# Slot two's weights behind the first gathers, and a new order around the first two expert slots

## The reference

```python
gl = (x @ p['w_rg']).astype(jnp.float32) + p['b_rg'].astype(jnp.float32)
gp_sel, gsel = lax.top_k(jax.nn.softmax(gl, axis=-1), 1)
el = (x @ p['w_re']).astype(jnp.float32) + p['b_re'].astype(jnp.float32)
...
topv, topi = lax.top_k(ep, TOP_K_IN_GROUP)
...
g = jnp.einsum('nd,edf->nef', x, p['w_e_gate'])
u = jnp.einsum('nd,edf->nef', x, p['w_e_up'])
act = jax.nn.silu(g) * u * combine[:, :, None]
out = jnp.einsum('nef,efd->nd', act, p['w_e_down'])
```

## Time and profile before

| | us |
|---|---|
| median of 3 runs | 731.97 (730.36 to 732.15) |
| the profiled execution, whole | 733.88 |
| its span in the trace | 732.0 |
| TensorE busy in it | 696.0 (95%) |
| VectorE, ScalarE, GpSimd busy | 540.6, 346.7, 211.5 |

### The profile page before, as it was taken

The page is one execution under the profiler, slowest core; times in us unless marked ns, Lnnn a source line. Parts: engine busy times, 40 slices in busy tenths (PEclk is TensorE's granted clock), DMA queues, the critical chain, the costliest instruction groups (busy, mean ns, idle before and its releaser), DMA issues.

```text
span 732.0 us, 11123 instructions
## 1 busy us (share of the span) xinstructions
PE 696.0 (95%) x4409; PEld 606.8 (83%) x4409; DVE 540.6 (74%) x782; ACT 346.7 (47%) x455; POOL 211.5 (29%) x89
## 2 busy tenths in 40 slices
PE   5899999999999999999999999999879999999985
PEld 2489989999898898999999999887358888887762
DVE  3546999999858865865465564556789999878887
ACT  4542232432333443555276031125468888777644
POOL 3004323222200000000000000000129999889486
PEclk9899999999999999999999999999799999999998
DMA  9944244555615357441133434375948999989865
GB/s 321 377 149 145 83 173 173 173 174 186 233 57 91 49 124 127 34 144 58 60 120 96 143 115 138 121 259 203 420 166 332 397 404 409 419 325 383 322 240 205
DMA packets 75607, 149.10 MB, mean 204 GB/s; under 512 B 11302, under 2 KB 54626, under 8 KB 68836
## 3 DMA queue, kind: packets, MB, share of 16 engines
q1 hardware_dynamic: 61572, 125.28, 50.1%
q10 hardware_dynamic: 10096, 12.63, 4.8%
q0 software_dynamic: 3888, 10.49, 4.1%
HBM read 138.29 MB, written 20.05 MB: 216 GB/s over the span
## 4 chain that ended last, share of the span: by engine, by line
PE 57%; DVE 22%; DMA 8%; issue 5%; POOL 4%; ACT 2%; SPq 2%; POOLq 0%; DVEq 0%; ACTq 0%
PE psum L1015 19%; DVE psum L2095 14%; PE psum L1291 8%; PE psum L1333 7%; DMA down_raw<-in_w_e_down 4%; PE psum L514 3%; PE psum L515 3%; PE psum L520 3%; PE psum L950 3%; DMA w_more<-in_w_ada 2%; DMA xg<-h_d,slot_b 2%; PE psum L1034 1%; PE psum L1167 1%; SPq L813 1%; POOL down_l L732 1%
## 5 line engine op out<-in xcount | busy, mean ns | idle before, releaser
L1015 PE MATMUL psum<-hh,w_h 128*128 128x320 f32 x608 | 145.1, 320 | 0.2 <-issue 0.2
L1015 PE MATMUL psum<-hl,w_h 128*128 128x320 f32 x608 | 138.9, 310 | 0.0
L1015 PE MATMUL psum<-hh,w_l 128*128 128x320 f32 x608 | 138.8, 310 | 0.0
L1015 PEld LDWEIGHTS psum<-hh,w_h 128*128 128x128 f32 x608 | 100.1, 189 | 6.1 <-issue 3.6
L2095 DVE SCALAR_TENSOR_TENSOR psum<-conv,taps,psum 128x760 f32<-128x760 f32 x100 | 101.5, 1015 | 3.4
L1015 PEld LDWEIGHTS psum<-hl,w_h 128*128 128x128 f32 x608 | 102.0, 188 | 0.0
L1015 PEld LDWEIGHTS psum<-hh,w_l 128*128 128x128 f32 x608 | 102.0, 189 | 0.0
L698 POOL TENSOR_TENSOR ob<-obh,toff 128x260 bf16<-128x260 f32 x1 | 2.0, 1994 | 331.8 <-DVE obh L606 331.8
L732 POOL TENSOR_TENSOR down_l<-down_raw,down_h 128x2048 fp32r<-128x2048 f32 x16 | 87.1, 5444 | 21.7 <-ACT down_h L1851 21.4
L2386 DVE TENSOR_TENSOR w_l<-w_raw,w_h 128x2048 fp32r<-128x2048 f32 x26 | 76.0, 2927 | 12.4 <-ACT w_h L1857 12.4
L942 POOL TENSOR_TENSOR w_l<-w_raw,w_h 128x2048 fp32r<-128x2048 f32 x9 | 42.1, 4680 | 142.3 <-ACT w_h L1532 142.3
(11 more groups left out here) (384 smaller groups left out, 1397.8 us busy)
## 6 DMA issues: line engine op xcount, KB each, us to landing
w_raw<-in_w_in SPq DMA_DIRECT2D x20, 1024.0 KB, 6.3
down_raw<-in_w_e_down SPq DMA_DIRECT2D x17, 1024.0 KB, 16.5
w_raw<-in_w_ada SPq DMA_DIRECT2D x16, 1024.0 KB, 9.7
w_raw<-in_w_e_gate SPq DMA_DIRECT2D x13, 1024.0 KB, 9.0
w_raw<-in_w_e_up SPq DMA_DIRECT2D x13, 1024.0 KB, 11.7
w_more<-in_w_ada SPq DMA_DIRECT2D x8, 1024.0 KB, 10.0
y_d<-yy ACTq DMA_DIRECT2D x15, 512.0 KB, 8.1
y_d<-in_x_sample SPq DMA_DIRECT2D x12, 512.0 KB, 8.8
```

The costliest lines, as they stand in the source:

```text
L1015: mm = pe.matmul(psum[:, p + q, 0:HALF], w, r[:, k, q * HALF:(q + 1) * HALF], start=(k == 0 and x == 0), stop=(k == KT - 1 and x == 2))
```

## The change

Six edits, all around the first slots:

1. SyncE: slot 2's gate and up weights are asked for after the `h2` stores and after both first gathers have landed, where they were asked for ahead of the down weights of slots 1 and 0. Slot 2's down weights follow them, so they now wait for the gathers too.
2. TensorE, slot 0: the rows of slot 1 are turned after slot 0's sixteen high products, where they were turned before them.
3. ScalarE: one Silu on a constant right after the router's two exponentials, and slot 1's two high weights ahead of the copies of `bg2`, where they were made inside slot 0.
4. VectorE: slot 0's second low weight after the two `x_low`, and slot 1's first low weight ahead of slot 1's `x_low`.
5. VectorE: the reduction to `wslot` stays ahead of slot 0 (`late_weights`); the thirteen other instructions of `late_tables` run after slot 0.
6. The count of slots is announced by the second step of semaphore `tables`.

```diff
+    def late_weights(dve):
+        dve.wait_ge(rt_pe, 3)
+        dve.tensor_reduce(wslot[:, :], psum[:, 6, 4 * NS:7 * NS].rearrange("p (k n) -> p n k", k=3), AX, ADD).then_inc(tables, 1)
+        dve.wait_ge(tables, 1)
+
     def late_tables(dve, then):
...
-        dve.wait_ge(rt_pe, 3)
-        then(dve.tensor_reduce(wslot[:, :], psum[:, 6, 4 * NS:7 * NS].rearrange("p (k n) -> p n k", k=3), AX, ADD))
         then(dve.scalar_tensor_tensor(out=pair_of(6), in0=pair_of(2), scalar=float(CAP), in1=places, op0=MUL, op1=ADD))
...
# SyncE
-        gate_up(2, 0, own(2))
         sp.wait_ge(x2_done, NT)
         down_weights(1, 1, own(1))
         sp.wait_ge(lg_done, 1)
         down_weights(0, 0, own(0))
         sp.wait_ge(h2_st, 16 * (NT + 1))
+        for s in range(2):
+            sp.wait_ge(xg_in[s], 16)
+        gate_up(2, 0, own(2))
         down_weights(2, 0, own(2))
...
# TensorE, slot
-            if not last:
+            if not first and not last:
                 turn_x(1 - s, u + s, b + 1)
...
             with_high(pe, psum[:, s, :], [(xh[:, s, k, :], xl[:, s, k, :], both(wh, k)) for k in range(KT)])
+            if first:
+                turn_x(1, 0, 1)
             pe.wait_ge(e_lo, 2 * b + 2)
...
# ScalarE
+        act.activation(rms[:, 31:32], ones[:, 0:1], ACT.Silu)
         gate2_rows(1)
+        for c in range(2):
+            w_hi(1, 1, 0, c)
...
-            if not last:
+            if early > 0 and not last:
                 for c in range(2):
                     w_hi(1 - s, b + 1, u + s, c)
...
# VectorE
-        for c in range(2):
-            w_lo(0, 0, c)
+        w_lo(0, 0, 0)
         x_low(0, 0, 0)
         x_low(0, 0, 1)
-        late_tables(dve, then)
+        w_lo(0, 0, 1)
+        late_weights(dve)
...
+            if early == 0:
+                w_lo(1, 1, 0)
             if not last:
                 for q in range(2):
                     x_low(1 - s, b + 1, q)
+            if early > 0 and not last:
                 w_lo(1 - s, b + 1, 0)
...
-        for b in range(LOOP_AT):
+        slot(0, 0, 0)
+        late_tables(dve, then)
+        for b in range(1, LOOP_AT):
             slot(b, b % 2, b // 2)
```

More of the change, by code:

```diff
@@ L668, in pair_count @@
     def pair_count(eng):
-        eng.wait_ge(tables, 1)
+        eng.wait_ge(tables, 2)
         return eng.value_load(pairs_i[0:1, 0:1], min_val=0, max_val=(OVER - 1) // 2) + NE // 2
```

## The result

The changed kernel takes 735.27 us (median of 5 runs, 734.44 to 740.83) where the kernel before takes 730.70 (5 runs, 730.26 to 732.15): a ratio of 1.0087, 95% interval 1.0064 to 1.0109, slower by 4.6 us. 737.5 had been forecast, slower with 0.76.

A forecast was written before the change was run, and what follows sets the result against it. TensorE, busy 95%, was taken as the bound, with VectorE and GpSimd excluding each other in slots 1 and 2. 7.0 - 2.95 + 1.5 = 5.55 us slower gave 739.4 profiled, 737.5 on the 731.97 median; range 731.0 to 740.3.

The forecast's parts named there:

- The hold: Behind slot 0, GpSimd's down-weight subtraction goes first and holds the first of VectorE's thirteen table instructions until S + 7.61.
- S: Start of slot 0's Silu on ScalarE: 545.54 us before, predicted 2.95 us earlier, at 542.6.
- two operands in SBUF: Reason given for the hold: tiny VectorE instructions reading two SBUF operands wait for GpSimd's subtraction, as at 694.45 (3.42 us).
- GpSimd's second subtraction: For slot 1, ready at S + 10.2, goes ahead of VectorE's first low weight of slot 2, until S + 14.8.
- 7.0: Loss in us at slot 1's activation turns on TensorE, against S: S + 17.4 instead of S + 10.41.
- No further loss from slot 3 on: Sign that the prediction is right: the slots from 3 on lose nothing more.
- The gather's 2.5 us: First gather lands at 533.2 instead of rows reaching TensorE at 535.75: gain 2.5 us, bounds nothing to 2.86.
- The turns behind the products: Slot 0 on TensorE: 1.1 us saved by turning slot 1's rows later, 0.9 coming back between high and low products.
- The clock's 1.5 us: TensorE's clock falls to 0.50 somewhere between 553 and 565 us, costing 1.5 us.
- two waits that were predicted: TensorE idle about 2.8 us ahead of slot 0's down products and about 4 us ahead of slot 1's activation turns.
- the rival without a hold: Tiny instructions aren't held behind slot 0, TensorE bounds, full 2.95 us gained: 729.0 us; chance 0.14.
- 4.05 + 1.5: Whole predicted loss, 5.55 us: 7.0 lost against S less its 2.95 gain, plus 1.5 for the clock.

The follow-up runs named there:

- GpSimd after the tables: Changed kernel, with GpSimd's first subtraction for the down weights made to wait until the thirteen table instructions are done: 734.81 us, ratio 1.0078.
- only the tables moved: Kernel before, with only the thirteen table instructions moved behind slot 0 (and edit 6, which goes with it): 737.27 us, ratio 1.0110.
- only weights moved: Kernel before, with only slot 2's three weights asked for behind the first gathers: 730.26 us, ratio 1.0015.
- six tables late: Changed kernel, with seven table instructions ahead of slot 0's first turns and six (a reduction, a minimum, four casts) behind slot 0: 731.77 us, ratio 1.0033.
- down weight late: Kernel of tables in the wait, with slot 2's gate and up weights asked for at their old place again: 730.55 us, ratio 0.9997.
- seven products: Kernel of tables in the wait, plus seven products of constants on TensorE ahead of slot 0's first product: 732.64 us, ratio 1.0033.
- tables in the wait: Changed kernel, with the thirteen table instructions back ahead of slot 0's products, between its first low weight and low tokens: 730.72 us, ratio 1.0017.
- clock at the products: Kernel of down weight late, plus five products of constants while TensorE waits for the rounded rows ahead of slot 0's first product: 730.64 us, ratio 1.0002.
- four casts late: Changed kernel, with nine table instructions ahead of slot 0's first turns and only the four casts behind slot 0: 733.22 us, ratio 1.0034.

## Why the prediction was right, and where it was not

1. **The hold, the step on which the sign rested: right.** The first of the thirteen lasted 4.56 us instead of 0.17 and ended with GpSimd, the tables were done at S + 10.03 (S + 10.15 predicted). The two runs that put only these instructions in the one place or the other move the time by 4.5 us (changed kernel) and 6.9 us (kernel before). Freeing these instructions of the hold is not enough, though: in the run with GpSimd after the tables they weren't held, two low weights were, and the loss stayed. The reason given, two operands in SBUF, was too narrow: a minimum with a constant and a cast were held as well, a reduction was not. The Trainium skill ("SBUF — State Buffer", section "SBUF: two separate sides") names VectorE instructions in a two-port mode beside those with two SBUF inputs, and I had used only the second. That the minimum and the cast were held (4.28 and 4.61 us) fits the first, but no row here shows in which mode they ran.

2. **GpSimd's second subtraction: the right collision at the wrong instruction.** Predicted ahead of slot 2's first low weight, slot 1's turns then at S + 17.4. In the run with only the tables moved it is so (S + 17.30). In the changed kernel slot 1's products began later, behind the third gather, and at a clock of 0.58 (see 5.); slot 1's Silu came at S + 10.24 instead of S + 7.9, and VectorE had begun the first low weight when GpSimd was ready. Slot 1's turns came at S + 14.21; the second low weight was held instead (6.30 us), and slot 2's turns came at S + 26.14, 6.40 us later than before against S (566.64 - 540.50, and 565.28 - 545.54 before; the row of 565.28 is):

```profile
565.28 0.39 PE L950 MATMUL psum<-ident,act 128*128 128x128 f32 x2
```

7.0 had been predicted, for slot 1's turns, which were only 3.80 late. "No further loss from slot 3 on" holds, but slot 2 itself had its share.

3. **The gather's 2.5 us: mis-sized.** The first turns came 1.02 us earlier against G (5.63 after it, 6.65 before). The gather was no longer the last to come: TensorE's own eight products of the scale rows took 6.33 us at the clock of 0.50, and the turns waited 0.47 us for what ScalarE makes of them. Before, the clock rose at 530 us, in the midst of these products, and they took 4.96; after, the low stretch was longer, 13.7 us instead of 10.2 (515.3 to 529.0, and 519.6 to 529.9), for a reason that no run shows. In other kernels of this set these products took 4.92 to 5.50 us, and the first turns came 4.56 to 4.84 us after G (only weights moved, six tables late, down weight late, seven products): 1.8 to 2.1 of the 2.5 us were there to be had. I had taken the landing of the gather for the wait's end, and not asked what else would be late by then.

4. **The turns behind the products: right.** From the first turns to S it is 9.79 us before and 9.41 after; 0.45 less was predicted with the clock. With 3., S gains 1.40 us instead of 2.95.

5. **The clock's 1.5 us: at the wrong place.** No low stretch came between 553 and 565 us; TensorE's waits from 550 to 567 us were 0.22, 0.76, 1.14 and 0.87 us. (Of the two waits that were predicted, 2.8 and 4.2 us, the first wasn't longer than both of those seen before, as the text has it: one of them is 2.86.) It came at 542 to 546 us, behind the wait for slot 0's activation and a third gather 0.52 us late. That gather was issued at 533.01, among slot 2's 3 MB (issued from 532.67 to 533.94), and took 9.4 us to land; the prediction had the lateness of the weights in view, at no cost, and not that of the gather beside them. The low clock's cost lay largely beside the hold: TensorE waited 0.22 us for `al` where 2.8 was predicted.

The sum at slot 2 is 6.40 - 1.40 = 5.00 us, 4.05 + 1.5 = 5.55 in the prediction; at slot 12 4.29 is left, at the end 4.44. That the two sums lie so close is luck in part: the clock's 1.5 us, which didn't come where they were placed, stand in the sum for the 1.55 us of S's gain that stayed out. The forecast of 737.5 came from 731.97 for the kernel before; on the 730.70 of the longer comparison the same sum gives 736.25, 1 us above what was measured. That the rival without a hold was given 729.0 (the full gain of S kept) was wrong too: the run with the tables in the wait is the nearest to that case, and kept nothing of it that can be measured.

What stays open: what takes, between slot 9 and the end, the lead of 1.5 to 2.3 us that three of the kernels with unheld tables have at slot 2 (tables in the wait, only weights moved, clock at the products). The waits speak for transfers taking part up to slot 12; behind slot 16 something else takes the lead, and what that is isn't shown.

## What to carry to other kernels

Here small bookkeeping instructions on VectorE cost only their own length where GpSimd wasn't at a long subtraction from SBUF, and the rest of that subtraction where it was. Put them into a wait of VectorE, and look at which instruction of GpSimd becomes ready just before the place. When a transfer is moved to make another arrive earlier, find the second-latest thing that the waiting instruction needs, since the gain ends there. And a lead at the start of a pipeline need not reach its end: read the waits of the later slots, and of what follows them, before adding it to the sum.

## What the runs showed of the hardware that was not expected

- One-operand VectorE instructions of 128x10 and 128x16 elements, a minimum with a constant and a cast to int32, are held by GpSimd's subtraction for 4.28 and 4.61 us; a reduction from SBUF beside the same subtraction took 0.31 us.
- GpSimd's gather takes part in this too: 2.88 us at 551.93 in the run with GpSimd after the tables, and 2.88 at 553.30 in the kernel before, both ending 0.88 us after a low weight of VectorE; 1.19 at 525.46 in the changed kernel, with no low weight beside it. GpSimd's next subtraction followed each of the two at once. In the one kernel VectorE's next low weight then took 7.37 us, in the other GpSimd's subtraction took 6.18, with the same starts against each other within 0.02 us.
- Where GpSimd waited already when an instruction of VectorE ended, and VectorE's next was one that can be held, GpSimd went first in each case shown here (at 543.52 after, at 543.52 with only the tables moved, at 545.06 with four casts late). Where VectorE's next was one that isn't held (the activation product at 554.17 after, the reduction at 542.24 with six late), it ran beside GpSimd's subtraction, and the one behind it was held.
- A low stretch of TensorE's clock moved with the waits: behind 2.19 us for the picks in the changed kernel, behind 1.82 us for the rounded rows with the down weight late, behind 3.51 us for `ob` when the wait for the picks was filled.
